# Values of three heads computed ahead of the heads, and the end of a head run among the next head's first tiles

## What is computed

```python
hn = rmsnorm(h, g_norm[l]); proj = hn @ w_in[l]
aq, ak, av, ag, bq, bk, bv, bg, mq, mg = jnp.split(proj, IN_SPLITS, axis=-1)
a_out = swa_sink_attention(aq, ak, av, sinks, a_slopes)   # band of 128 keys, 8 heads of 64, 2 key heads
# B, 4 heads: two maps of 64-wide queries and keys, values 128 wide, chunk-causal
logits = einsum('bqchd,bschd->bchqs', qb, k) * scale - slopes * dist      # masked
p = softmax(logits); attn = p[:, 0] - lam * p[:, 1]; b_heads = attn @ v
b_out = rmsnorm(b_heads, b_subln_g[l]) * (1.0 - lam_init)
# M, 4 heads: 256 memory tokens
m_out = softmax(mq @ mk.T * d ** -0.5) @ mv
gated = concatenate([a_out * silu(ag), b_out * silu(bg), m_out * silu(mg)], -1)
h = h + gated @ w_out[l]
return rmsnorm(h, g_final)
```

## Time and profile before

| | us |
|---|---|
| median of 3 runs (lowest, highest) | 702.26 (701.86, 703.21) |
| the profiled execution, device time | 703.01 |
| its span in the trace | 701.2 |
| PE busy | 692.0 (99%) |
| DVE, ACT, POOL busy | 418.0, 313.4, 231.2 |
| granted TensorE clock over the span | 1.0 of full (the 2.4 GHz level) |

### The profile page before, as it was taken

One profiled execution on the slowest core, in us unless ns is written; L12 is line 12 of the kernel. 1 busy time (PEld: TensorE's weight loads), 2 busy tenths in 40 slices (PEclk: granted clock), 3 DMA queues, 4 the chain that ended last, 5 costly groups with the idle time before them and its releaser, 6 DMA issues.

```text
span 701.2 us, 11598 instructions
## 1 busy us (share of the span) xinstructions
PE 692.0 (99%) x3933; PEld 580.4 (83%) x3933; DVE 418.0 (60%) x916; ACT 313.4 (45%) x733; POOL 231.2 (33%) x204
## 2 busy tenths in 40 slices
PE   8999999999999999999999999999999999999996
PEld 8888888888888888888888888788888888888885
DVE  6786246766753666675457677735666786633332
ACT  6763444455543445564334646434454654222200
POOL 4723132144332214343231434232234542322310
PEclk9999999999999999999999999999999999999999
DMA  9921212020052111105211110421140285514210
GB/s 298 310 62 31 61 31 61 1 59 3 1 150 61 32 30 33 29 1 150 61 31 31 31 31 1 142 68 31 31 124 2 65 243 175 168 60 131 82 58 36
DMA packets 79157, 52.73 MB, mean 75 GB/s; under 512 B 36080, under 2 KB 71936, under 8 KB 79104
## 3 DMA queue, kind: packets, MB, share of 16 engines
q1 hardware_dynamic: 79104, 52.06, 26.1%
HBM read 43.14 MB, written 8.91 MB: 74 GB/s over the span
## 4 chain that ended last, share of the span: by engine, by line
PE 95%; DVE 3%; issue 1%; ACT 0%; DVEq 0%; POOL 0%; POOLq 0%; ACTq 0%
PE acc L1497 17%; PE acc L1498 17%; PE acc L1499 17%; PE score L1497 5%; PE score L1499 5%; PE score L1498 5%; PE trans L1499 3%; PE trans L1497 3%; PE trans L1498 3%; PE score L1702 2%; PE score L1704 2%; PE trans L1722 2%; PE mixo L1498 2%; PE mixo L1499 2%; PE mixo L1497 2%; PE score L1781 1%
## 5 line engine op out<-in xcount | busy, mean ns | idle before, releaser
L1497 PE MATMUL acc<-x_hi,w_hi 128*128 128x512 f32 x512 | 204.2, 399 | 0.2 <-DVE gates L1265 0.2
L1498 PE MATMUL acc<-x_lo,w_hi 128*128 128x512 f32 x512 | 200.2, 391 | 0.0
L1499 PE MATMUL acc<-x_hi,w_lo 128*128 128x512 f32 x512 | 199.9, 390 | 0.0
L942 POOL TENSOR_TENSOR w_lo<-w_raw,w_hi 128x512 fp32r<-128x512 f32 x66 | 85.0, 1308 | 174.4 <-ACT w_hi L610 156.6
L1499 PEld LDWEIGHTS acc<-x_hi,w_lo 128*128 128x128 f32 x512 | 96.1, 188 | 20.7
L1497 PEld LDWEIGHTS acc<-x_hi,w_hi 128*128 128x128 f32 x512 | 96.3, 188 | 19.5 <-issue 1.8
L1498 PEld LDWEIGHTS acc<-x_lo,w_hi 128*128 128x128 f32 x512 | 96.4, 188 | 16.8
L789 ACT ACTIVATE logits<-logits,stats_b 128x128 f32<-128x128 f32 (+7 forms) x64 | 49.2, 770 | 50.5 <-DVE stats_b L1294 50.5
L1286 DVE CUSTOM_DVE_ANT_0 logits<-score,b_bias 128x384 f32<-128x384 f32 (+5 forms) x96 | 49.8, 554 | 23.2 <-PE score L1704 22.6
L798 ACT ACTIVATE p_hi<-trans 128x512 fp32r<-128x512 f32 (+1 forms) x56 | 30.8, 565 | 63.4 <-PE trans L1722 42.1
L1313 DVE TENSOR_TENSOR p_lo<-trans,p_hi 128x512 fp32r<-128x512 f32 (+1 forms) x56 | 35.8, 651 | 33.6 <-ACT p_hi L798 33.1
(11 more groups left out here) (254 smaller groups left out, 1398.4 us busy)
## 6 DMA issues: line engine op xcount, KB each, us to landing
w_raw<-in_w_in SPq DMA_DIRECT2D x68, 256.0 KB, 3.4
mixed<-gates SPq DMA_DIRECT2D x9, 512.0 KB, 4.2
mix_raw<-mixed SPq DMA_DIRECT2D x8, 576.0 KB, 5.9
wo_raw<-in_w_out SPq DMA_DIRECT2D x8, 512.0 KB, 6.7
x_res<-in_x SPq DMA_DIRECT2D x8, 512.0 KB, 3.3
out_y<-y_row SPq DMA_DIRECT2D x16, 256.0 KB, 2.1
logits<-in_x SPq DMA_DIRECT2D x4, 512.0 KB, 7.4
wo_raw<-in_w_out SPq DMA_DIRECT2D x6, 256.0 KB, 5.9
```

The lines of the kernel that those rows point to most:

```text
L942: last = pool.tensor_tensor(w_lo[:, slot, cols], w_raw[:, slot, cols], w_hi[:, slot, cols].bitcast(F32), ALU.subtract)
L1497: pe.matmul(out, a_hi, b_hi, start=start, stop=False, skip_group_check=True)
L1498: pe.matmul(out, a_hi, b_lo, start=False, stop=False, skip_group_check=True)
L1499: return pe.matmul(out, a_lo, b_hi, start=False, stop=stop, skip_group_check=True)
```

## The change

- **Values ahead.** The tile bv leaves heads 0 to 2 (`TILES` has seven); head 3 keeps it (`TILES_LAST`). The values of heads 0 to 2 (384 columns) are computed behind the preparation, in four value tiles: two k-tiles each, for each of eight blocks of 128 rows of x, with x as the stationary operand and 384 columns of w_in moving, 192 matmuls 128x384 in all. Each row block has one of the eight PSUM banks (`v_banks`). They come out rows first, so no `v_spread` is needed. ACT and DVE copy four banks each, SP stores them to DRAM (`values`, eight DMAs) and loads a head's 128 columns back into `b_out`; at (3,0,2) `v_split` splits them, on ACT (high) and POOL (`v_lo`, remainder), two halves of 128x512 each.
- **The end of a head** (what stood behind the quarters of tile 7, and b_gate) is now the table `BEHIND`, and stands among tiles 0 and 1 of the next head, ahead of the evacuation where both stand behind one quarter. Both `b_finish` stand at (0,1,1), ahead of the evacuation of the second half of the keys. Head 3 keeps its end behind its own tile 7.
- **Roots and Exp.** Behind the second square root ACT does one Exp of one column (`exp_ahead`).
- **Memory's keys and values** go to DRAM once (`mem_kv`) and each head's part is loaded to `mk_in`, `mv_in`; their split (`mkv`) stands at (2,1,0) in place of the head's start. The split queries of M (`q_m_hi`, `q_m_lo`) lie over `mk_raw` and `mv_raw` instead of over `q_b`.
- **`b_scores 4 1`** goes from the first place behind (4,0,0) to the last behind (3,1,2). `b_squares 0` goes behind `a_scores 3`.
- **Loops** of heads are written out on every engine. On SP, in the last head the load of `mix_raw` 0 goes behind all scores and behind the loads of wo 1 and 2.

```diff
-TILES = [("bk", BK, True), ("bq", BQ, True), ("bv", BV, False), ("aq", AQ, True),
-         ("ag", AG, True), ("mq", MQ, False), ("mg", MG, False), ("bg", BG, False)]
+TILES = [("bk", BK, True), ("bq", BQ, True), ("aq", AQ, True), ("ag", AG, True), ("mq", MQ, False),
+         ("mg", MG, False), ("bg", BG, False)]
+TILES_LAST = TILES[0:2] + [("bv", BV, False)] + TILES[2:]
...
+    (2, 1, 0): [("mkv",)],
     (2, 1, 1): [("b_combine", 1)],
...
+BEHIND = {
+    (0, 0, 0): [("m_scores", 3), ("b_fold", 1)],
+    (0, 0, 1): [("a_mix", 2), ("m_norm", 3), ("m_spread", 2)],
+    (0, 0, 2): [("m_mix", 1), ("b_low", 1)],
+    (0, 0, 3): [("m_spread", 3), ("m_mix", 2)],
+    (0, 1, 0): [("a_spread", 3), ("m_mix", 3), ("b_squares", 1)],
+    (0, 1, 1): [("b_finish", 0), ("b_finish", 1)],
+    (0, 1, 2): [("a_mix", 3)],
+    (1, 0, 1): [("b_gate",)],
+}
...
-    (7, 1, 1): [("b_finish", 0)],
-    (7, 1, 2): [("b_finish", 1)],
-    (7, 1, 3): [("b_gate",), ("a_mix", 3)],
...
+                out.append((0, ("project", w, s, q)))
+                out += [(1, step) for step in BEHIND.get((w, s, q), [])]
+                if q == 3:
+                    out.append((0, ("evacuate", w, s)))
+                out += [(0, step) for step in between.get((w, s, q), [])]
...
+            def value_tile(n):
+
+                pe.wait_ge(w_lo_done, n + 1)
+                for t in range(ST):
...
+                    rows = slice(t * P, (t + 1) * P)
+                    for c in range(2):
+                        k = 2 * (n - OWN_TILES) + c
+                        cols = slice(c * HALF, c * HALF + AHEAD)
+                        last = product(v_banks[t][:, 0:AHEAD], x_hi[:, k, rows], x_lo[:, k, rows], w_hi[:, n % 2, cols],
+                                       w_lo[:, n % 2, cols], k == 0, k == KT - 1)
...
+                def mkv():
+                    act.wait_ge(mkv_loaded, 32 * (h + 1))
                     act.wait_ge(pt_done, h * NMIX)
...
+                    if s == 1 and h < HEADS - 1:
+                        act.activation(exp_ahead, eps, ACT.Exp)
...
+            for h in range(1, HEADS):
+                load_head_tile(2, h)
+                for g in "ma":
+                    spill(g, h - 1)
+                load_mem_kv(h)
+                load_head_tile(3, h)
+                spill("b", h - 1)
+                if h < HEADS - 1:
+                    load_values(h)
```

More of the change, by code:

```diff
@@ new lines, in numbered, with head_steps @@
+def numbered(*events):
+    return {key: n for n, key in enumerate(events)}
+def head_steps(tiles, between):
+    out = [(0, ("start",))]
+    for w in range(len(tiles)):
+        out.append((0, ("weights", w + 1)))
+        for s in range(2):
+            for q in range(4):
+                out.append((0, ("project", w, s, q)))
[3 more added lines that the diff above has]
+                out += [(0, step) for step in between.get((w, s, q), [])]
+    return out
@@ L87 @@
     (7, 0, 3): [("m_spread", 3), ("m_mix", 2)],
-    (7, 1, 0): [("a_spread", 3), ("m_mix", 3), ("b_squares", 1)],
-    (7, 1, 1): [("b_finish", 0)],
-    (7, 1, 2): [("b_finish", 1)],
-    (7, 1, 3): [("b_gate",), ("a_mix", 3)],
-}
-def numbered(*events):
-    return {key: n for n, key in enumerate(events)}
[L108 to L126, removed]
+    (7, 1, 0): [("a_spread", 3), ("m_mix", 3), ("b_squares", 1), ("mix_first", 0)],
     (7, 1, 1): [("wo_split", 1)],
@@ L893, in head @@
                         wo_hi_part(s[1])
-            with act.Fori(0, HEADS - 1) as h:
-                head(h, HEAD)
-            head(HEADS - 1, LAST)
+            for n in range(HEADS):
+                for h, order in in_order(n):
+                    head(h, order)
             def finish_row(par, z):
@@ L1045, in head @@
                             .then_inc(wo_lo_by_pool, 1)
-            with pool.Fori(0, HEADS - 1) as h:
-                head(h, HEAD)
-            head(HEADS - 1, LAST)
+            for n in range(HEADS):
+                for h, order in in_order(n):
+                    head(h, order)
             with pool.Fori(0, ST // 2 - 1) as z:
@@ L1457, in head @@
                         mix_mid_part(s[1])
-            with dve.Fori(0, HEADS - 1) as h:
-                head(h, HEAD)
-            head(HEADS - 1, LAST)
+            for n in range(HEADS):
+                for h, order in in_order(n):
+                    head(h, order)
             def finish(par, z):
@@ L1657, in _ @@
                 spread_shared(v)
+            for n in range(OWN_TILES, PRE_TILES):
+                value_tile(n)
             def head(h, order):
@@ L1837, in head @@
                         b_squares(s[1])
-            for h in range(HEADS - 1):
-                head(h, HEAD)
-            head(HEADS - 1, LAST)
-            w_out_hi = [w_hi[:, 0, :]] + [t[:, 0, :] for t in wo]
-            w_out_lo = [w_lo[:, 0, :]] + [t[:, 1, :] for t in wo]
+            for n in range(HEADS):
+                for h, order in in_order(n):
+                    head(h, order)
+            w_out_hi = [w_hi[:, 1, :]] + [t[:, 0, :] for t in wo]
+            w_out_lo = [w_lo[:, 1, :]] + [t[:, 1, :] for t in wo]
             def y_product(par, s, j):
```

383 lines of the change are left out of this document (270 added, 113 removed).

## The result

The changed kernel takes 714.27 us (711.83 to 716.04, 4 runs) where the kernel before takes 702.58 (701.86 to 703.21, 4 runs). The ratio is 1.0168, interval 1.0156 to 1.018: 11.7 us slower. The profiled execution has a span of 714.3 us and a device time of 716.04, the highest of the four.

What follows compares the result with a forecast made beforehand. PE, busy 692.0 of 701.2 us, was taken to bound the kernel. Terms -1.6 - 0.4 - 0.5 + 1.2 + 7.5 = +6.2 gave 709.2 profiled, 708.5 against the median; range 700.0 to 712.5.

Steps and rivals of the forecast that it cites:

- The keys' evacuation behind the roots: Second half of tile bq: PE waits for DVE's k_lo behind two reciprocals; +7.5 us over three boundaries (+6 to +10).
- The rule of the Trainium skill that was weighed there: DVE and GpSimd share a port pair by whole instructions; at its worst a boundary costs 4.5 us, the sum 13.5.
- Together 2.5 x 3 boundaries: Starts of three heads: 2.0 us wait for k_lo plus 0.5 for a multiplication meeting POOL, +7.5 us.
- a larger stall: Heads' boundaries: multiplications wait for whole POOL instructions, or SP loads late; 12 to 15, giving 713 to 716; chance 0.09.
- Scores of row block 4: Moved second piece, b_scores 4 1: a small PE wait at b_scores 5 0 is saved; -0.4 us (-1.4 to 0).
- It exchanges one small wait for another: Moved b_scores 4 1 needs a bank DVE frees at 114.85, PE there about 114.76; hence only -0.4 us.
- Memory's split between two combines: At (2,1,0): POOL's remainders delay b_combine 1's scaling and PE's transposes 0.25 to 0.4, four times; +1.2 us (0 to +2).
- Values ahead: Value matmuls ahead of the heads: 32.6 us removed, 33.6 added, transposes 2.6 saved; -1.6 us (-2.6 to -1.1).
- The formula that the prediction quotes from the Trainium skill: Matmul spacing of N/2.4 ns plus 2.5 ns: 0.216 us for 512 columns, 0.1625 for 384; values part about -2.5.
- Old waits: Heads' starts: PE waits behind DVE, some 0.3 us with restart in heads 1 and 3, go; -0.5 us (-0.6 to 0).
- The Exp: Behind the second root: moves a 1.3 us table load to where ACT waits for DVE; put at zero.
- No stall at the keys: Second half of tile bq: k_lo done before PE wants the bank, no wait; 701.0, or 699.8 with split hidden; chance 0.17.

Runs made afterwards that it cites:

- finish_late: Changed kernel with the second b_finish moved from (0,1,1) to (1,0,0) of the next head; 705.66 us, ratio 1.0049 to the kernel before.
- waits of 8.8: Changed kernel with the second b_finish's reciprocal done three times in heads 0 to 2; 736.71 us, ratio 1.0495 to the kernel before.
- three of 1.30: Changed kernel with the first b_finish's reciprocal over half its columns in heads 0 to 2; 708.13 us, ratio 1.0085 to the kernel before.
- before_scores_moved: Kernel before with b_scores 4 1 moved as in the change, nothing else; 701.82 us, ratio 0.9998.
- finish_late_scores_back: finish_late with b_scores 4 1 back as the first step behind (4,0,0); 703.03 us, ratio 1.0009 to the kernel before.
- finish_late_mkv_late: finish_late with the split of the memory's keys and values at (3,1,0) instead of (2,1,0); 703.77 us, ratio 1.0023 to the kernel before.

## Why the prediction was wrong

The direction was right and the size was not: +6.2 was forecast for the profiled execution, +13.0 came, and 714.3 lies above the range of 700.0 to 712.5. Two steps failed, one that isn't in the sum at all and one with the wrong sign; without either one the median would have been inside the range. The one run with a clock of 0.999, 711.83, is.

- **The keys' evacuation behind the roots: right.** The chain was worked out to end 2.0 late, and 0.5 was added for the multiplication that meets POOL: 2.5 per boundary. The wait is 2.56, with its restart 2.72. The multiplication took 1.20 instead of 0.69, 0.51 more. finish_late shows the cause by taking it away. The rule of the Trainium skill that was weighed there ("SBUF — State Buffer", "🔬 SBUF: two separate sides") agrees with the trace in kind, and taken at its worst it would have been 2 us too much at each boundary.
- **What PE does after it has stood: missed (3.4 of the 6.8).** The step that failed is "Together 2.5 x 3 boundaries": it priced the wait and nothing after it. The matmuls behind two of three waits ran at the 1.2 GHz level for 3.4 us, 1.7 us each. No row of before could show it, since PE never stood that long in its heads; no case stood for it, though "a larger stall" had its time. The Trainium skill says of it, in "TensorE: Matmul & The Clock Gate", section "HAM oscillation — how this bites in real kernels", that waits between bursts of matmuls send the clock back and the next burst begins at the low level. The traces agree for the waits of 8.8: behind all three the first matmul ran at the low level. For 2.55 they differ: the waits of the page's case are longer, and here the clock fell behind four of six, in three of them only 0.3 to 1.2 us after PE had begun again. Behind the three of 1.30 it didn't fall.
- **Scores of row block 4: the wrong sign (2.9 of the 6.8).** -0.4 was forecast, +2.5 came. "It exchanges one small wait for another" looked at PE's and DVE's part of the step alone. The step of that size that was taken off there is 0.18 us in rows 2 and not 0.16, which changes the term by less than 0.1. The step also holds ACT's exponentials of the block (1.6 us), and the tile behind which it stands had changed from one that ACT doesn't touch to one it does. before_scores_moved and finish_late_scores_back together show it.
- **Memory's split between two combines: right**, +1.2 forecast. The gaps were 0.28 to 0.35, 1.2 in four heads, and finish_late_mkv_late takes them away.
- **Values ahead: right**, -1.6 forecast, -1.9 measured. A matmul 128x384 took 33.39/192 = 0.174 us, between the two bounds. Nothing waits for the supply, the loads or `v_split`, as put at zero. No run has this part by itself; the figure is read from the spacing. The formula that the prediction quotes from the Trainium skill ("TensorE: Matmul & The Clock Gate", section "Back-to-back issue gap") is there the gap of an isolated matmul and not of a stream; the measured spacing decided, as the prediction said.
- **Old waits: -0.5 forecast**, about -1.2 with the single slips, which are at other places in each trace. **The Exp: zero, right.**
- **The rivals.** "No stall at the keys" didn't come. "A larger stall" had the time, 713 to 716, by another mechanism than it named: neither the multiplications' wait nor SP. With 0.09 on it and the range cut below it, the range had no room for two small misses of the same sign.

## What to carry to other kernels

When a step is moved in one list that all engines follow, write down what each engine does in it and which evacuation it now stands ahead of: the costs of this change were a DVE reciprocal ahead of one evacuation, ACT's exponentials ahead of another and POOL's remainders ahead of a scaling. All three went when the step was put behind the instruction that PE waits for, and with the gate of B moved too the change gained 0.3%. A new wait of PE can have a second price, the low clock behind it: here 1.7 us, four times of six, on a wait of 2.55.

## What the runs showed that was not expected

- With waits of 2.55 the clock falls to 0.50 for some 3.4 us: once 0.2 us before PE begins again, and in the other three cases 0.3, 1.1 and 1.2 us after, while PE is fully busy. With a wait of 8.8 it falls during the wait and is low at the first matmul. Behind four of six waits of 2.55 it fell, behind none of three of 1.30. No run has a wait between these lengths.
- A table load on ACT went ahead of the wait of the activation that needs it: 1.28 us at 235.93, with the activation at 238.71, and alike in the next two heads. In this kernel the table could be left to load itself, since ACT is idle before its first use.
